# Encoder layer with expert-choice MoE: the experts' first two weights cut into blocks of 1024 columns instead of 352

## What is computed

```python
def expert_choice_moe(h, router_w, w1, w3, w2):
    ...
    gates, idx = lax.top_k(aff.T, cap)      # cap = 2 * tokens / 16: 32 and 64 tokens

    def expert(args):
        w1e, w3e, w2e, ie, ge = args
        xe = jnp.take(xt, ie, axis=0)
        hid = jax.nn.silu(xe @ w1e) * (xe @ w3e)
        return (hid @ w2e).astype(jnp.float32) * ge[:, None]

    ye = lax.map(expert, (w1, w3, w2, idx, gates))
    out = jnp.zeros((n, D), jnp.float32).at[idx.reshape(-1)].add(ye.reshape(-1, D))
```

## Time and profile before

| | |
|---|---|
| median of 3 runs | 2223.64 us (2223.26 to 2223.94) |
| profiled execution, its own time | 2221.62 us |
| its span | 2219.8 us |
| granted TensorE clock, mean | 0.976 |
| TensorE matmuls busy | 93% of the span, 12268 instructions |
| TensorE weight loads busy | 82% |
| VectorE busy | 73% |
| ScalarE busy | 61% |
| moved by DMA | 618.30 MB |
| share of TensorE in the chain that ended last | 64% |

### The profile page before, as it was taken

The page is one execution under the profiler, slowest core; times in us unless marked ns, Lnnn a source line. Parts: engine busy times, 40 slices in busy tenths (PEclk is TensorE's granted clock), DMA queues, the critical chain, the costliest instruction groups (busy, mean ns, idle before and its releaser), DMA issues.

```text
span 2219.8 us, 31309 instructions
## 1 busy us (share of the span) xinstructions
PE 2057.7 (93%) x12268; PEld 1829.6 (82%) x12268; DVE 1626.3 (73%) x1249; ACT 1357.4 (61%) x1127; POOL 70.9 (3%) x38
## 2 busy tenths in 40 slices
PE   3999997767949999999999999999999999999998
PEld 2899997635739798888979889897988989798896
DVE  3235664576358888888888888788888888888886
ACT  4223342364137777777777767777777777777674
POOL 0000000000020001000000000000000000000000
PEclk9999999788979999999999999999999999999999
DMA  4113223021649999999999999999999999999994
GB/s 156 59 49 93 75 75 121 27 88 35 220 152 319 346 385 342 379 354 371 372 360 384 346 371 363 370 373 353 383 349 374 362 369 374 354 383 349 371 368 169
DMA packets 354900, 618.30 MB, mean 279 GB/s; under 512 B 12448, under 2 KB 299168, under 8 KB 354848
## 3 DMA queue, kind: packets, MB, share of 16 engines
q1 hardware_dynamic: 351264, 604.99, 76.6%
q0 software_dynamic: 3584, 12.58, 2.5%
HBM read 597.09 MB, written 20.45 MB: 278 GB/s over the span
## 4 chain that ended last, share of the span: by engine, by line
PE 64%; ACT 6%; issue 3%; DVE 2%; DMA 1%; SPq 0%; ACTq 0%; POOL 0%; DVEq 0%; POOLq 0%
PE pair L479 20%; PE pair L477 20%; PE pair L478 20%; ACT chunk_high L973 3%; PE pair L767 1%; DMA hg<-projected 1%; ACT L983 1%; ACT L973 1%; PE pair L697 1%; PE pair L721 0%; ACT y_rows L999 0%; DVE hid L1400 0%; ACT silu L983 0%; DVE top_tokens L1358 0%; DVE top_values L1356 0%
## 5 line engine op out<-in xcount | busy, mean ns | idle before, releaser
L1388 DVE TENSOR_TENSOR chunk_low<-ring,chunk_high 128x2816 fp32r<-128x2816 f32 (+1 forms) x382 | 1179.3, 3091 | 254.0 <-ACT chunk_high L973 250.8
L973 ACT ACTIVATE chunk_high<-ring 128x2816 fp32r<-128x2816 f32 (+2 forms) x384 | 980.8, 2558 | 189.8 <-PE pair L479 189.6
L477 PE MATMUL pair<-chunk_high,xe_high 128*96 128x352 f32 x2048 | 666.0, 325 | 10.3 <-DVE chunk_low L1388 9.1
L479 PE MATMUL pair<-chunk_high,xe_low 128*96 128x352 f32 x2048 | 666.9, 326 | 0.0
L478 PE MATMUL pair<-chunk_low,xe_high 128*96 128x352 f32 x2048 | 659.7, 322 | 0.0
L477 PEld LDWEIGHTS pair<-chunk_high,xe_high 128*96 128x96 f32 x2048 | 330.2, 161 | 22.2 <-issue 21.1
L478 PEld LDWEIGHTS pair<-chunk_low,xe_high 128*96 128x96 f32 x2048 | 330.9, 162 | 6.2
L479 PEld LDWEIGHTS pair<-chunk_high,xe_low 128*96 128x96 f32 x2048 | 330.2, 161 | 0.2
L477 PE MATMUL pair<-chunk_high,hid_high 128*96 128x512 f32 x704 | 279.4, 397 | 0.0
L479 PE MATMUL pair<-chunk_high,hid_low 128*96 128x512 f32 x704 | 276.7, 393 | 0.0
L478 PE MATMUL pair<-chunk_low,hid_high 128*96 128x512 f32 x704 | 275.9, 392 | 0.0
(11 more groups left out here) (200 smaller groups left out, 1886.4 us busy)
## 6 DMA issues: line engine op xcount, KB each, us to landing
ring<-w SPq DMA_DIRECT2D x256, 1408.0 KB, 9.9
ring<-w SPq DMA_DIRECT2D x96, 1536.0 KB, 10.5
ring<-w SPq DMA_DIRECT2D x32, 1024.0 KB, 7.8
raw_w<-w_in SPq DMA_DIRECT2D x16, 1024.0 KB, 5.8
projected<-stage SPq DMA_DIRECT2D x60, 128.0 KB, 1.7
wo_raw<-w_out SPq DMA_DIRECT2D x8, 512.0 KB, 3.2
x_in<-x SPq DMA_DIRECT2D x6, 512.0 KB, 7.3
qk<-projected SPq DMA_DIRECT2D x6, 512.0 KB, 3.8
```

The lines of the kernel that those rows point to most:

```text
L477: pe.matmul(dst, a_high, b_high, start=first, stop=False)
L479: return pe.matmul(dst, a_low, b_high, start=False, stop=last)
L973: act.activation(ch[c % SPLIT][:, 0:n], ring[c % RING][:, 0:n], ACT.Copy).then_inc(ch_done, 1)
L1388: dve.tensor_tensor(cl[c % SPLIT][:, 0:n], ring[c % RING][:, 0:n], ch[c % SPLIT][:, 0:n].bitcast(F32), ALU.subtract).then_inc(cl_done, 1)
```

## The change

`w1` and `w3` are cut into three blocks of columns, 1024, 1024 and 768 wide. A block of 1024 goes in three chunks of 3, 3 and 2 row tiles, a block of 768 in two chunks of 4, first all of `w1`'s, then all of `w3`'s. That is again 16 chunks, with moving operands of 512 columns (and of 512 and 256 in the last block): 240 matmuls of 512 columns and 48 of 256 for an expert, in place of 384 of 352. The partial sums of a block of `w1` fill both banks of `PA`, those of `w3` both of `PB`; there is no second set. `silu` is written into `hid` itself, once for each block, and the product replaces it there. The transposes of a block's first half come behind the second chunk after its last one, those of the second half behind the third. `W2_KT` is 3, 2, 3, 3, 3, 2, 3, 3, so two short chunks do not follow each other any more. The next expert's rows are transposed behind chunks 19 and 20.

```diff
 FT = FF // P
 CAP_P, CAP_S = 2 * PROMPT // EXPERTS, 2 * SAMPLE // EXPERTS
 SLOTS = CAP_P + CAP_S
-FC = 352
-NFC = FF // FC
-W2_KT = [3, 3, 3, 3, 3, 3, 2, 2]
+BLOCK_W = [1024, 1024, 768]
+BLOCK_AT = [0, 1024, 2048]
+BLOCK_KT = [[3, 3, 2], [3, 3, 2], [4, 4]]
+NB = len(BLOCK_W)
+UP = [(b, m, sum(BLOCK_KT[b][:i]), n) for b in range(NB) for m in range(2) for i, n in enumerate(BLOCK_KT[b])]
+W2_KT = [3, 2, 3, 3, 3, 2, 3, 3]
 W2_AT = [sum(W2_KT[:j]) for j in range(len(W2_KT))]
-CHUNKS = 2 * NFC + len(W2_KT)
+CHUNKS = len(UP) + len(W2_KT)
+FIRST = {(b, m): min(c for c, u in enumerate(UP) if u[:2] == (b, m)) for b in range(NB) for m in range(2)}
+LAST = {(b, m): max(c for c, u in enumerate(UP) if u[:2] == (b, m)) for b in range(NB) for m in range(2)}
 RING = 6
 SPLIT = 3
 EARLY = 2
 CHUNK = 3 * D
-TILES_AFTER = [FC * (c + 1) // P for c in range(NFC)]
-T_PER_EXPERT = NFC + 2
+HALVES = [[(BLOCK_AT[b] // P + g * BLOCK_W[b] // (2 * P), BLOCK_W[b] // (2 * P)) for g in range(2)] for b in range(NB)]
+HID_AT = {LAST[b, 1] + 2 + g: (b, g) for b in range(NB) for g in range(2)}
+XE_AT = {len(UP) + 3: 0, len(UP) + 4: 1}
+T_PER_EXPERT = 2 * NB + 2
...
     ring = [sb(moe, f"ring{i}", [P, CHUNK], side="right") for i in range(RING)]
-    silu = [sb(moe, f"silu{i}", [SLOTS, FC]) for i in range(2)]
...
     y_sb = sb(moe, "y_rows", [SLOTS, D])
-    ch = [sb(moe, f"chunk_high{i}", [P, CHUNK], F32R) for i in range(SPLIT)]
+    ch = [sb(moe, f"chunk_high{i}", [P, CHUNK], F32R) for i in (2, 0, 1)]
+    ch = ch[1:] + ch[:1]
     cl = [sb(moe, f"chunk_low{i}", [P, CHUNK], F32R) for i in range(SPLIT)]
...
     def chunk_view(buf, c):
 
-        if c < 2 * NFC:
-            return buf[:, 0:KT * FC].rearrange("p (k n) -> p k n", k=KT)
-        k = W2_KT[c - 2 * NFC]
-        return buf[:, 0:k * D].rearrange("p (k n) -> p k n", k=k)
+        k, n = (UP[c][3], BLOCK_W[UP[c][0]]) if c < len(UP) else (W2_KT[c - len(UP)], D)
+        return buf[:, 0:k * n].rearrange("p (k n) -> p k n", k=k)
 
     def chunk_size(c):
-        return KT * FC if c < 2 * NFC else W2_KT[c - 2 * NFC] * D
+        return UP[c][3] * BLOCK_W[UP[c][0]] if c < len(UP) else W2_KT[c - len(UP)] * D
 
     def load_chunk(sp, e, c, ahead=0):
 
-        if c < 2 * NFC:
-            w, c0 = (w1, w3)[c % 2], c // 2 * FC
-            src = w.rearrange("e d n -> (e d) n")[bass.ds(e * D + ahead * D, D), c0:c0 + FC]
+        if c < len(UP):
+            b, m, k0, n = UP[c]
+            src = (w1, w3)[m].rearrange("e d n -> (e d) n")[bass.ds(e * D + (ahead * D + k0 * P), n * P),
+                                                            BLOCK_AT[b]:BLOCK_AT[b] + BLOCK_W[b]]
         else:
-            j = c - 2 * NFC
+            j = c - len(UP)
             src = w2.rearrange("e f n -> (e f) n")[bass.ds(e * FF + (ahead * FF + W2_AT[j] * P), W2_KT[j] * P), :]
...
         def expert(e, last):
-            def hid_tiles(fc):
-                return range(TILES_AFTER[fc - 1] if fc else 0, TILES_AFTER[fc])
-
             for c in range(CHUNKS):
                 pe.wait_ge(cl_done, e * CHUNKS + (c + 1))
                 hi, lo = chunk_view(ch[c % SPLIT], c), chunk_view(cl[c % SPLIT], c)
-                if c < 2 * NFC:
-                    fc = c // 2
+                if c < len(UP):
+                    b, m, k0, n = UP[c]
                     if c == 0:
                         pe.wait_ge(tl_done, e * T_PER_EXPERT + 2)
-                    if c % 2 == 0:
-                        pe.wait_ge(hid_done, e * NFC + (fc + 1))
-                    dst = (H1, H3)[c % 2][fc % 2][0:SLOTS, 0:FC]
-                    for k in range(KT):
-                        mm = split_mm(dst, xeh[:, k, :], xel[:, k, :], hi[:, k, :], lo[:, k, :],
-                                      k == 0, k == KT - 1)
+                    if c == FIRST[b, 0]:
+                        pe.wait_ge(silu_done, e * NB + (b + 1))
+                    if c == FIRST[b, 1]:
+                        pe.wait_ge(hid_done, e * NB + (b + 1))
+                    for k in range(n):
+                        for c0 in range(0, BLOCK_W[b], 512):
+                            cols = slice(c0, min(c0 + 512, BLOCK_W[b]))
+                            mm = split_mm((PA, PB)[m][0:SLOTS, cols], xeh[:, k0 + k, :], xel[:, k0 + k, :],
+                                          hi[:, k, cols], lo[:, k, cols], k0 + k == 0, k0 + k == KT - 1)
                 else:
-                    j = c - 2 * NFC
+                    j = c - len(UP)
                     if j == 0:
                         pe.wait_ge(y_ev, e + 1)
-                    if j == len(W2_KT) - 2:
-                        pe.wait_ge(tl_done, e * T_PER_EXPERT + (2 + NFC))
-                    elif j == 0:
-                        pe.wait_ge(tl_done, e * T_PER_EXPERT + (1 + NFC))
+                        pe.wait_ge(tl_done, e * T_PER_EXPERT + (2 + 4))
+                    if W2_AT[j] <= HALVES[2][0][0] < W2_AT[j] + W2_KT[j]:
+                        pe.wait_ge(tl_done, e * T_PER_EXPERT + (2 + 5))
+                    if W2_AT[j] <= HALVES[2][1][0] < W2_AT[j] + W2_KT[j]:
+                        pe.wait_ge(tl_done, e * T_PER_EXPERT + (2 + 6))
...
-                if c >= 2 and c % 2 == 0 and c // 2 - 1 < NFC:
-                    fc = c // 2 - 1
-                    pe.wait_ge(hid_done, e * NFC + (fc + 3))
-                    pe.wait_ge(tl_done, e * T_PER_EXPERT + (1 + fc))
-                    for i, k in enumerate(hid_tiles(fc)):
-                        mm = pe.transpose(TB[fc % 2][:, i * SLOTS:(i + 1) * SLOTS], hid[:, tile(k)],
+                if c in HID_AT:
+                    b, g = HID_AT[c]
+                    k0, n = HALVES[b][g]
+                    pe.wait_ge(hid_done, e * NB + (b + 2))
+                    pe.wait_ge(tl_done, e * T_PER_EXPERT + (1 + 2 * b + g))
+                    for i in range(n):
+                        mm = pe.transpose(TB[g][:, i * SLOTS:(i + 1) * SLOTS], hid[:, tile(k0 + i)],
                                           ident[0:SLOTS, 0:SLOTS])
                     mm.then_inc(t_mm, 1)
-                if not last and c in (2 * NFC + 2, 2 * NFC + 3):
-                    j = c - 2 * NFC - 2
-                    pe.wait_ge(tl_done, e * T_PER_EXPERT + (1 + NFC + j))
-                    transpose_rows(j, e * 16 + 32)
+                if not last and c in XE_AT:
+                    pe.wait_ge(tl_done, e * T_PER_EXPERT + (1 + 2 * NB + XE_AT[c]))
+                    transpose_rows(XE_AT[c], e * 16 + 32)
 
...
                 c = cc - 2
-                if c % 2 == 0 and c < 2 * NFC:
-                    fc = c // 2
+                if c < len(UP) and c == LAST[UP[c][0], 0]:
+                    b = UP[c][0]
                     act.wait_ge(used, e * CHUNKS + (c + 1 + SPLIT))
-                    act.activation(silu[fc % 2][:, :], H1[fc % 2][0:SLOTS, 0:FC], ACT.Silu).then_inc(silu_done, 1)
-                if c >= 2 and c % 2 == 0 and c // 2 - 1 < NFC:
-                    fc = c // 2 - 1
-                    k0, k1 = (TILES_AFTER[fc - 1] if fc else 0), TILES_AFTER[fc]
-                    act.wait_ge(t_mm, e * T_PER_EXPERT + (3 + fc))
-                    act.activation(hid_h[:, k0:k1, :],
-                                   TB[fc % 2][:, 0:(k1 - k0) * SLOTS].rearrange("p (k n) -> p k n", k=k1 - k0),
+                    act.activation(hid[:, BLOCK_AT[b]:BLOCK_AT[b] + BLOCK_W[b]], PA[0:SLOTS, 0:BLOCK_W[b]],
+                                   ACT.Silu).then_inc(silu_done, 1)
+                if c in HID_AT:
+                    b, g = HID_AT[c]
+                    k0, n = HALVES[b][g]
+                    act.wait_ge(t_mm, e * T_PER_EXPERT + (3 + 2 * b + g))
+                    act.activation(hid_h[:, k0:k0 + n, :], TB[g][:, 0:n * SLOTS].rearrange("p (k n) -> p k n", k=n),
                                    ACT.Copy).then_inc(th_done, 1)
-                if not last and c in (2 * NFC + 2, 2 * NFC + 3):
-                    j = c - 2 * NFC - 2
-                    rows_high(j, e * T_PER_EXPERT + (3 + NFC + j))
+                if not last and c in XE_AT:
+                    rows_high(XE_AT[c], e * T_PER_EXPERT + (3 + 2 * NB + XE_AT[c]))
...
+        act.sem_inc(silu_done, 1)
...
                 c = cc - 2
-                if c % 2 == 1 and c < 2 * NFC:
-                    fc = c // 2
-                    dve.wait_ge(silu_done, e * NFC + (fc + 1))
+                if c < len(UP) and c == LAST[UP[c][0], 1]:
+                    b = UP[c][0]
+                    own = hid[:, BLOCK_AT[b]:BLOCK_AT[b] + BLOCK_W[b]]
+                    dve.wait_ge(silu_done, e * NB + (b + 2))
                     dve.wait_ge(used, e * CHUNKS + (c + 1 + SPLIT))
-                    dve.tensor_tensor(hid[:, fc * FC:(fc + 1) * FC], H3[fc % 2][0:SLOTS, 0:FC], silu[fc % 2][:, :],
-                                      ALU.mult).then_inc(hid_done, 1)
-                if c >= 2 and c % 2 == 0 and c // 2 - 1 < NFC:
-                    fc = c // 2 - 1
```

(22 more changed lines are left out.)

## The result

| | before | changed |
|---|---|---|
| median | 2223.45 us (4 runs) | 2185.00 us (4 runs, 2182.69 to 2185.16) |
| ratio | | 0.9827, 95% interval 0.9812 to 0.9841 |
| profiled execution's span | 2219.8 us | 2180.9 us |
| one expert in the loop | 96.66 us | 93.98 us |
| the last expert, end to end on TensorE | 94.21 us | 93.30 us |

A forecast was written before the change was run, and what follows sets the result against it. TensorE was taken to bound the experts, with three stalls from ScalarE and VectorE. Savings of 11.7 + 8.4 + 15.4 + 1.4 - 2.1 = 34.8 us gave 2186.8, or 2189 us on the median's scale; range 2183 to 2210.

The forecast's parts named there:

- Wider matmuls: TensorE's matmuls for `w1` and `w3`, 512 and 256 columns instead of 352: 0.73 us saved an expert, 11.7 us in all.
- Short chunks apart: Ahead of chunk 0: reordered `W2_KT` removes the stall, 0.57 us in 14 looped experts, 0.40 in the last, 8.4 in all.
- Chunk 2 short and Silu behind chunk 4: Ahead of chunk 2: ready at 7.31 us, before chunks 0 and 1 end at 8.31, so the 0.39 us stall goes.
- Next late is chunk 3: At chunk 3's start: start possible at 11.15 us, wanted at 11.08, so 0.07 us lost.
- Transposes two chunks later: Ahead of a block's first transposes: product wanted 8.3 us behind the block's end, needs some 5; the 0.71 us stall goes.
- 1.67 + 0.10: Per looped expert on TensorE: three late starts lose 1.67 us together, and restarts some 0.10 us beyond those gaps.
- the 0.15 put down for new stalls and the loop boundary: Cost at newly tight chunks 3 and 23 and the loop boundary: 0.15 us an expert, 2.1 us over 14.
- the 94.2 to 94.5 that was named as the sign of being right: Time of one expert, in us, that would show the forecast right.
- the case at the low end of the range: Whole kernel at 2183 us: nothing lost at the new tight places, late starts worth 0.2 us beyond their gaps.
- The chain of parts: Rival, chance 0.06: ScalarE's and VectorE's high and low parts set the pace, 6.2 us lost an expert, about 2283 us.
- The weight-load floor: Rival, chance 0.03: weight loads hold 256-column matmuls to 0.161 us instead of 0.119, 32 us in all, 2221, no change.
- Loads as the bound: Rival, chance 0.03: all weight DMA at 368 GB/s takes 96.2 us an expert, about 2216 us.

## Why the prediction was right, and where it was not

**Wider matmuls** (0.73 us an expert, 11.7 in all): measured 0.82 in the loop (94.80 to 93.98) and 0.91 in the last expert (94.21 to 93.30). The size was nearly right. The reason given for it, a fixed part of 7.6 ns a matmul, was not: it was drawn through 352 and 512 columns, and the 256-column run gives 3.7. By the line through 256 and 512 columns a matmul of 352 should take 0.444 x 352 + 3.7 = 160 ns, and it takes 161.1. So less than half of the saving is the fixed part of 96 matmuls (0.36 us), and the rest is a nanosecond or so, on average, in each of the 384 of that width. The excess sits at one place. In an expert of the run with no table loads and short chunks apart, the mean distances inside a product's three matmuls are 159 and 160 ns, and 164 from its third matmul to the next product's first (165 in 98 of 120 cases); at 512 columns the three are 231, 230 and 231 in the changed kernel. Why is open; that 161 ns is also the duration of a weight load was noticed and not tried. By the rule of the Trainium skill, "TensorE: Matmul & The Clock Gate", section "Back-to-back issue gap", the step would be 96 x 2.5 ns = 0.24 us an expert (the prediction has 0.26) and the sum 2196, as an estimate; the 2185.00 measured does not bear that out.

**Short chunks apart** (8.4 us): wrong as a term of its own. Alone it gave 0.5 us, which is within what a measurement can tell. The prediction said itself that chunk 2 is ready 8.76 us behind the end of chunk 23, and then added the stall ahead of chunk 0 to the one ahead of chunk 2 as if the first did not shorten the second. Beside the removal of the table loads it gave 0.70 an expert, and undoing it in the changed kernel cost 1.06 ahead of chunk 0.

**Chunk 2 short and Silu behind chunk 4** (0.39 an expert): its true size is the whole 1.02 that is left when chunk 0 is on time, and with the long chunk 2 the changed kernel is slower than the kernel before. What the later place of Silu and of the second table load is worth without the short chunk was not measured. "Next late is chunk 3" held in that the margin there is gone (the weight load shows 0.18), but the matmul lost nothing, and chunk 23 is just as close (0.17).

**Transposes two chunks later** (0.71 an expert): this stall too was part of the others. In the kernel before, moving the transposes alone gave 0.48, since 0.21 was chunk 3's lateness; and without the table loads the stall was gone with the transposes where they had always been. In the changed kernel the second chunk is needed all the same, for another reason: the product of 1024 columns ends later behind its block, and one chunk less costs 0.71 and 0.69 at the two wide blocks. That this is the forecast's number is chance.

**The total** came out because all terms were removed at once: the late starts are one chain of deadlines, and its sum, 1.67 and what is lost right behind them, is what goes when the last of them goes. The prediction had 1.67 + 0.10 and the runs give 1.86. An expert of the loop was to gain 0.73 + 1.67 + 0.10 - 0.15 = 2.35 and gained 2.68: 0.09 more by the wider matmuls, 0.09 more by the late starts, and the 0.15 put down for new stalls and the loop boundary did not appear (0.23 between starts in the loop). Over 14 experts that is 4.6 us more. The last gained 0.2 more than forecast. The first gained nothing where 0.73 was forecast, since TensorE begins it 0.68 later (at 665.24 instead of 664.56). 34.8 + 4.6 + 0.2 - 0.8 = 38.8, the difference of the spans. So an expert's 93.98 lies below the 94.2 to 94.5 that was named as the sign of being right; it is the case at the low end of the range, nothing lost at the new places and 0.2 beyond the gaps. The agreement of the total thus says less than it seems to: two of its terms, short chunks apart and the transposes, are not worth their figures by themselves, and the total is right because the stalls were added up whole.

**The rivals.** The chain of parts did not become the pace: no round makes TensorE wait in the changed kernel. With chunks 2 and 5 long, two places of an expert were late, and not every round. The weight-load floor is excluded by 0.1173 us for 256 columns. Loads as the bound are excluded for pieces of 1280 to 1536 bytes and shown for 1024.

## What to carry to other kernels

Stalls on one engine that hang on the same queue of another are not terms of a sum. Take each as a deadline counted from one common event (here TensorE's end of chunk 23), and see which is late when the others are met. A version of each step alone is no test of its worth in the whole, in either direction: here a reordering was worth nothing in the loop alone and 0.7 to 1.1 us an expert beside the other steps. Where a queue has a slow spot (here `y_rows` and a table load), try the shortest piece of work right behind it.
